# Expert down matrices stored slot by slot, with the two half tiles of neighbouring groups joined

## What is computed

```python
def expert(args):
    xe, wg, wu, wd = args              # 32 x 1024, 1024 x 2816, 1024 x 2816, 2816 x 1024
    a = jnp.einsum('bcd,df->bcf', xe, wg)
    u = jnp.einsum('bcd,df->bcf', xe, wu)
    return jnp.einsum('bcf,fd->bcd', jax.nn.silu(a) * u, wd)

out = lax.map(expert, (xin, w_gate, w_up, w_down))
```

## Time and profile before

| What | Value |
|---|---|
| Median of 3 runs | 2984.71 us |
| Lowest and highest run | 2976.73 and 2993.71 us |
| Span of the profiled execution | 2981.8 us |
| TensorE busy | 2348.0 us, 79% of the span |
| HBM read | 752.11 MB, 253 GB/s over the span |

### The profile page before, as it was taken

How to read it: one execution, slowest core, us unless ns; L and a number is a source line. 1 busy time by engine, 2 the same in 40 slices (tenths; PEclk the granted TensorE clock), 3 DMA queues, 4 the chain that set the end, 5 groups by cost and what they waited for, 6 DMA issues and landing times.

```text
span 2981.8 us, 36065 instructions
## 1 busy us (share of the span) xinstructions
PE 2348.0 (79%) x15206; PEld 1421.3 (48%) x15206; DVE 874.7 (29%) x1463; ACT 594.1 (20%) x964; POOL 63.1 (2%) x58
## 2 busy tenths in 40 slices
PE   6967767666666666777666789985899999868998
PEld 3844211111111111111111269972599799866997
DVE  6453000000000000000000044478455455554544
ACT  2410100000000000000000034410244454433443
POOL 0010000000000000000000000005100000000000
PEclk9977755555555555555555689996999999889999
DMA  5033899999999999999999955413245254321440
GB/s 219 15 145 137 293 387 402 392 373 371 370 391 394 390 372 377 374 396 401 368 380 374 390 224 190 147 37 155 85 170 183 105 223 180 142 120 64 173 180 32
DMA packets 110804, 754.27 MB, mean 253 GB/s; under 512 B 10791, under 2 KB 10952, under 8 KB 63432
## 3 DMA queue, kind: packets, MB, share of 16 engines
q1 hardware_dynamic: 107712, 748.20, 66.2%
q10 hardware_dynamic: 3016, 5.00, 0.5%
HBM read 752.11 MB, written 1.05 MB: 253 GB/s over the span
## 4 chain that ended last, share of the span: by engine, by line
PE 44%; DMA 27%; SPq 18%; DVE 8%; issue 1%; ACT 1%; POOL 0%; DVEq 0%; POOLq 0%; ACTq 0%
PE ps L1270 17%; SPq L963 11%; DMA work<-in_w_down 9%; DMA work<-in_w_gate 8%; PE ps L1281 8%; DMA work<-in_w_up 6%; SPq L966 5%; PE ps L773 3%; PE ps L423 2%; SPq L958 2%; PE ps L1836 2%; PE ps L988 2%; PE ps L1704 1%; PE ps L1013 1%; DMA ring<-in_w_up 1%
## 5 line engine op out<-in xcount | busy, mean ns | idle before, releaser
L988 PE MATMUL ps<-ring,arena 128*32 128x352 f32 x3072 | 452.9, 736 | 189.4 <-DMA ring<-in_w_gate 102.7
L1270 PEld LDWEIGHTS ps<-hsplit,w 128*128 128x128 f32 x4224 | 517.6, 192 | 6.2
L1270 PE MATMUL ps<-hsplit,w 128*128 128x256 f32 x4224 | 520.2, 283 | 0.0
L988 PEld LDWEIGHTS ps<-ring,arena 128*32 128x32 f32 x3072 | 110.1, 150 | 525.3 <-DMA ring<-in_w_gate 194.6
L1030 ACT ACTIVATE arena<-ps 128x352 f32<-128x352 f32 x32 | 13.1, 461 | 1312.1 <-PE ps L988 1312.1
L1040 DVE TENSOR_TENSOR arena<-arena,ps 128x352 f32<-128x352 f32 x32 | 15.2, 518 | 829.7 <-ACT arena L1030 829.7
L1281 PE MATMUL ps<-w,hidsplit 128*128 128x512 f32 x1056 | 255.3, 391 | 0.0
L1013 PE MATMUL ps<-work,arena 128*32 128x256 f32 (+1 forms) x1536 | 160.8, 567 | 104.0 <-DMA work<-in_w_down 103.9
L1013 PE MATMUL ps<-ring,arena 128*32 128x256 f32 (+1 forms) x1536 | 171.2, 597 | 76.0 <-DMA ring<-in_w_down 65.7
L1341 DVE TENSOR_TENSOR w<-ring,w 128x1024 fp32r<-128x1024 f32 x176 | 214.4, 1222 | 43.8 <-ACT w L1304 43.8
L1281 PEld LDWEIGHTS ps<-w,hidsplit 128*128 128x128 f32 x1056 | 192.9, 188 | 36.6
(11 more groups left out here) (379 smaller groups left out, 2112.5 us busy)
## 6 DMA issues: line engine op xcount, KB each, us to landing
ring<-in_w_gate SPq DMA_DIRECT2D x96, 1408.0 KB, 29.9
ring<-in_w_up SPq DMA_DIRECT2D x96, 1408.0 KB, 34.7
ring<-in_ffn_w SPq DMA_DIRECT2D x88, 1536.0 KB, 6.4
ring<-in_w_down SPq DMA_DIRECT2D x32, 1536.0 KB, 23.7
work<-in_w_down SPq DMA_DIRECT2D x32, 1536.0 KB, 24.5
work<-in_w_up SPq DMA_DIRECT2D x32, 1408.0 KB, 31.2
work<-in_w_gate SPq DMA_DIRECT2D x32, 1408.0 KB, 32.5
work<-in_w_down SPq DMA_DIRECT2D x32, 1024.0 KB, 23.0
```

The costliest lines, as they stand in the source:

```text
L988: last = pe.matmul(k.ps[32 * g:32 * g + CAP, 2 * w + half, 0:FH], xe[:, kk, :], slot(k, base + n)[:, g * FG + half * FH:g * FG + (half + 1 ...
L1270: last = pe.matmul(k.ps[:, 4 + c % 4, w * S:(w + 1) * S], k.w13[:, b, w, i, kk, :], k.hsplit[:, j, kk, :], start=(kk == 0 and n == 0), sto ...
```

## The change

The down matrices are laid out anew before the kernel starts (in `laid_out`, on the host's side, where other weights were laid out already). The half tile of group 0 and that of group 1 become one tile of 128 rows, and so do those of groups 2 and 3, so that an expert has 22 tiles where it had 24. They are dealt to eight slots with 3, 3, 3, 3, 3, 3, 2 and 2 tiles, and for each slot the bytes of a partition lie side by side: one run of 12,288 (or 8,192) bytes per partition, and one transfer per slot. TensorE gets one more transpose, VectorE one more copy of 64 x 96, both to have the second half of the joined tile's weights at partitions 64 to 127 of `hidT`, and the down product runs over 22 tiles. The bytes read are the same.

```diff
+DOWN_TILES = []
+for _g in (0, 2):
+    DOWN_TILES += [(_h, _m) for _h in (_g, _g + 1) for _m in range(FT)] + [(_g, FT)]
+DOWN_SLOTS = [(0, 3), (3, 3), (6, 3), (9, 3), (12, 3), (15, 3), (18, 2), (20, 2)]
...
-                    g, part = (n - 2 * DK) // 2, n % 2
-                    rows = FG * g + 3 * P * part
-                    whole = 3 - part
-                    sync.dma_start(s[:, 0:whole * D].rearrange("p (m d) -> p m d", m=whole),
-                                   w_down[0, bass.ds(e, 1), rows:rows + whole * P, :].rearrange("e (m p) d -> p (e m) d", p=P)).then_inc(ready, 16)
-                    if part:
-                        sync.dma_start(s[0:FR, 2 * D:3 * D],
-                                       w_down[0, bass.ds(e, 1), rows + 2 * P:rows + 2 * P + FR, :].rearrange("e p d -> p (e d)")).then_inc(ready, 16)
+                    first, tiles = DOWN_SLOTS[n - 2 * DK]
+                    sync.dma_start(s[:, 0:tiles * D], w_down[bass.ds(e, 1), first * P * D:(first + tiles) * P * D]
+                                   .rearrange("e (p f) -> p (e f)", p=P)).then_inc(ready, 16)
...
+            last = pe.transpose(k.ps[:, 5, 2 * P:3 * P], hidden[:, FG - P:FG], k.ident)
             last.then_inc(turned, 1)
...
-            for g in range(NG):
-                for m in range(FT + 1):
-                    n = 2 * DK + 2 * g + m // 3
-                    if m % 3 == 0:
-                        pe.wait_ge(k.ready(base + n), e * again[n] + mark[n])
-                    w = P if m < FT else FR
+            for n, (first, tiles) in enumerate(DOWN_SLOTS, 2 * DK):
+                pe.wait_ge(k.ready(base + n), e * again[n] + mark[n])
+                for i in range(first, first + tiles):
+                    g, m = DOWN_TILES[i]
                     for j in range(NG):
-                        last = pe.matmul(k.ps[32 * j:32 * j + CAP, 6, 0:256], hidT[0:w, m, 32 * g:32 * g + CAP],
...
+                        last = pe.matmul(k.ps[32 * j:32 * j + CAP, 6, 0:256], hidT[:, m, 32 * g:32 * g + CAP],
...
-                dve.tensor_copy(hidT[0:FR, 5, :], k.ps[0:FR, 5, P:2 * P]).then_inc(hidT_rest_put, 1)
+                dve.tensor_copy(hidT[0:FR, 5, :], k.ps[0:FR, 5, P:2 * P])
+                dve.tensor_copy(hidT[FR:P, 5, 0:P - CAP], k.ps[FR:P, 5, 2 * P + CAP:3 * P]).then_inc(hidT_rest_put, 1)
...
+    down = np.asarray(a["w_down"][0]).reshape(NE, NG, FG, D)
+    tiles = [down[:, g, m * P:(m + 1) * P] if m < FT else np.concatenate([down[:, g, FT * P:], down[:, g + 1, FT * P:]], 1)
+             for g, m in DOWN_TILES]
+    out["w_down"] = np.concatenate([np.stack(tiles[first:first + n], 2).reshape(NE, -1) for first, n in DOWN_SLOTS], 1)
```

More of the change, by code:

```diff
@@ L935, in experts @@
     per = 3 * DK
-    dmas = [1] * (2 * DK) + [1, 2] * NG
-    mark = [k.use.landing(base + n, dmas[n]) for n in range(per)]
-    again = [k.use.landing(base + per + n, dmas[n]) - mark[n] for n in range(per)]
+    mark = [k.use.landing(base + n) for n in range(per)]
+    again = [k.use.landing(base + per + n) - mark[n] for n in range(per)]
     for e in range(2, NE):
         for n in range(per):
-            k.use.landing(base + per * e + n, dmas[n])
+            k.use.landing(base + per * e + n)
     def load(sync):
@@ L1005, in expert @@
                 weighted_sums(k, pe, range(NG - 1))
-            for g in range(NG):
-                for m in range(FT + 1):
-                    n = 2 * DK + 2 * g + m // 3
-                    if m % 3 == 0:
-                        pe.wait_ge(k.ready(base + n), e * again[n] + mark[n])
-                    w = P if m < FT else FR
-                    for j in range(NG):
-                        last = pe.matmul(k.ps[32 * j:32 * j + CAP, 6, 0:256], hidT[0:w, m, 32 * g:32 * g + CAP],
[L1014 to L1017, removed]
+            for n, (first, tiles) in enumerate(DOWN_SLOTS, 2 * DK):
+                pe.wait_ge(k.ready(base + n), e * again[n] + mark[n])
+                for i in range(first, first + tiles):
+                    g, m = DOWN_TILES[i]
+                    for j in range(NG):
+                        last = pe.matmul(k.ps[32 * j:32 * j + CAP, 6, 0:256], hidT[:, m, 32 * g:32 * g + CAP],
+                                         slot(k, base + n)[:, (i - first) * D + j * 256:(i - first) * D + (j + 1) * 256],
+                                         start=(i == 0), stop=(i == len(DOWN_TILES) - 1))
+                if n < per - 1:
+                    last.then_inc(k.slot_freed, 1)
             last.then_inc(down_done, 1)
@@ L2253, in laid_out @@
     return out
-WHOLE = ["x", "filt_w1", "filt_w2", "filt_w3", "w_out", "w_router", "w_gate", "w_up", "w_down", "final_norm_g",
+WHOLE = ["x", "filt_w1", "filt_w2", "filt_w3", "w_out", "w_router", "w_gate", "w_up", "final_norm_g",
          "ple_w_gate_2", "ab_w_in_2",
```

## The result

The changed kernel takes 2826.08 us (median of 4 runs, 2824.92 to 2831.03) against 2986.39 us for the kernel before in the same comparison: a ratio of 0.9475, with a 95% interval from 0.9438 to 0.9511 (the two medians alone give 0.9463). The forecast was 2835 us, in a range from 2815 to 2876. The profiled execution of it spans 2823.2 us, 158.6 us less than that of before.

A forecast was written before the change was run, and what follows sets the result against it. DMA was taken to bound the kernel; faster down transfers would save 9.6 us per expert, 153 us over 16, less 3 us for edges. That 150 us off the 2984.7 us median gave 2835 us, range 2815 to 2876.

The forecast's parts named there:

- The bound: Expert stage: it lasts as long as its bytes take on DMA; down matrix at 314 GB/s, gate and up at 425.
- Part 1: Down matrix's four 64-row transfers per expert: they slow themselves and transfers around them, and joining them removes the slow windows.
- The own price: A 64-row transfer by itself: 256 KB at 190 GB/s takes 0.76 us too much, 3.0 us per expert.
- The dips' price: Four slow windows in the first expert's down transfers, 237 to 281 GB/s against 412: 6.3 us lost.
- engines out of step: Around 64-row transfers: DMA engines sharing the way to a partition fall out of step and disturb each other's next transfer.
- Part 2: Down transfers: runs of 12,288 bytes in place of 4096 raise the rate to 425 GB/s, worth 0.7 us per expert.
- The sum: Both parts over the down matrix: 36.7 - 27.1 = 9.6 us per expert, 153 us over 16 experts.
- the 3 us taken off for edges: Expert stage: an allowance for edges such as the first transfers after a pause, leaving a gain of 150 us.
- Part 4: Between up and down: one more transpose and copy, at most 8.5 us in all, taken as nothing because the ring covers it.
- Only the price of the transfers themselves: Rival for the down transfers: only 3.0 us plus 0.7 us per expert goes, 59 us, to 2926 us; chance 7%.
- The dips go, the rest stays: Rival for the down matrix: 2.6 us per expert stay, gain 112 us, to 2873 us; chance 8%.
- Slower by contiguous blocks: Rival for the down transfers: 1.5 MB blocks are served badly; at 250 GB/s, 150 us more, 3135 us; chance 2%.

The follow-up runs named there:

- e1: The changed kernel with down matrices laid tile by tile, so runs are 4096 bytes again, with joined tiles and one transfer per slot kept; 2843.98 us, ratio to before 0.9525.
- e3: The kernel before with its 64-row transfers written to partitions 32 to 95, not 0 to 63, half tiles' part of the result left out; 2844.56 us, ratio 0.9525.
- e5: The changed kernel with every down slot sent as two 64-row transfers, partitions 0 to 63 and 64 to 127; 3428.27 us in 2 runs.
- e8: The changed kernel with each expert's last down slot sent as two 64-partition halves, SP waiting before and after them in the first expert only; 2946.92 us, single run.
- e7: The changed kernel with the added transpose between up and down done 21 times in place of once; 2831.33 us.

## Why the prediction was right

**The bound.** DMA, and the rate within an expert: right. The gate and up slots stayed at 3.39 us, and the down matrix now takes 81.33 - 54.2 = 27.1 us, the very value of the sum.

**Part 1, the 64-row transfers.** Right in kind, and shown by e1 and e3 from two sides. They cost (2982.68 - 2843.98) / 16 = 8.7 us per expert. The own price was put at 3.0 us, from a row of 190 GB/s; at the 218 GB/s of e5 it would be 2.3 us. The dips' price was put at 6.3 us, and 2.6 us were in no window. Most of those 2.6 us belonged to the same transfers. The earlier trace rows end the down phase at 1083 us and go on at 1089 us, and the stretch between is slow too:

```profile
1083.00:1089.00 6.00, 3.86 (x36) 1.17 (x32) 0.00 (x0) 0.00 (x0) 0.00 (x0) 0.50 1.00 346
```

The two stretches, 36 us at 331 and 6 us at 346 GB/s, lose 8.0 and 1.1 us against 425 GB/s, so 9.1 of the 9.6 us can be seen. The windows of the earlier trace rows have gaps and were held against 412 GB/s, which made the dips look smaller. The reason for the dips (engines out of step) was put as a reading; e5 and e8 support it and don't prove it.

**Part 2, the long runs.** Mis-sized: 0.7 us per expert in the sum, 1.0 to 1.1 us by e1 against the changed kernel. The clean windows of 3 and 4 us from which the 411 to 417 were read are too short for a difference of 1%. That long runs would be worth nothing, which the prediction set against its rows, is ruled out by the 17.9 us. Since the sum took both parts together from the whole 36.7 us, the error shifts 0.4 us between them and nothing in the total.

**The sum.** The 153 us were right, and the 3 us taken off for edges were not. The expert stage starts at 311.31 us before and at 306.56 us after, and the first turn of the next stage, at L1218, at 1752.37 and 1594.31 us:

```profile
306.56 6.12 PE L988 MATMUL ps<-ring,arena 128*32 128x352 f32 x80 [2.02 <-POOL arena L976]
...
1594.31 5.81 PE L1218 MATMUL ps<-arena 128*128 128x128 f32 x32 [0.71 <-ACTq L143]
```

for the changed kernel, and for the kernel before

```profile
311.31 6.12 PE L988 MATMUL ps<-ring,arena 128*32 128x352 f32 x80 [2.02 <-POOL arena L976]
...
1752.37 6.19 PE L1218 MATMUL ps<-arena 128*128 128x128 f32 x32 [0.71 <-ACTq L137]
```

The stretch between shrank from 1441.06 to 1287.75 us, by 153.3 us. Of the other 5.3 us of the difference of the spans, 4.75 us lie ahead of the experts, in code that the change doesn't touch; the forecast had no term for that part. Traces of other kernels came down on either side (e1 starts the stage at 310.9 us and e3, with the layout of before, at 306.5), so that isn't an effect of the layout; what makes it stays open. These 4.8 us and the 3 us are most of the 9 us by which 2835 was too high. The lower end of the range doesn't follow from its own terms: a down stream at 430 GB/s gives 5 us and the scatter 8 us, so 2822 us and not 2815. The measured time lies within either.

**Part 4, the added transpose and copy.** Right, and by e7 with much room.

**The rivals.** *Only the price of the transfers themselves* would have left 2926 us; by e1 the loss is 8.7 us per expert and not 3.0. e3 shows that the place of the 64 rows is the cause, and the size is three to four times what their own bytes at half rate give. *The dips go, the rest stays* (2873 us) didn't happen either: the down matrix fell to 27.1 us, so nothing stayed. *Slower by contiguous blocks* didn't happen: 425 GB/s for the whole stage.

## What to carry to other kernels

In a stage bound by DMA, take the rate of each kind of transfer apart, in windows of a few microseconds, and don't trust the DMA share: it is 1.0 for a stream at half rate too. A load of 64 rows at partition 0 (or 64) among full ones costs more than its own excess, here between one and a half times (e5) and three to four times (the kernel before) as much; join two such loads to one of 128 rows, or, where what reads them allows it, write them to partitions 32 to 95. Longer runs per partition come second (1.1 us of 82.4 here).

## What was not expected of the hardware

- Where 64 rows are written changes the time of a kernel by 138 us (4.6%) with the same transfers otherwise: partitions 0 to 63 against 32 to 95.
- One 1 MB slot per expert sent as two halves of 64 partitions costs 4.4 us in the fastest run and 7.8 us in the median, with a scatter of 2896 to 2965 us between runs, while kernels without 64-row transfers at partition 0 or 64 scatter by 5 to 9 us. The kernel before scatters by 17 us and, in the other comparisons, by 29 and 53 us. A stream with such transfers among full ones is not only slower, it is less even. And their price can grow within one execution, from 27.6 to 52.0 us per expert in e5.
- TensorE's granted clock in the down phase was higher with the faster stream, 0.87 where the earlier trace rows show 0.50:

```profile
1062.00:1090.00 28.00, 16.11 (x199) 7.88 (x199) 2.56 (x8) 1.88 (x2) 0.00 (x0) 0.87 1.01 425
```

The later three-tile down slots in the timeline above take 1.50 us, where the first still takes 2.79. The mean over the long stretch rose from 0.55 to 0.60 only. Why the clock rose was not tested. It bought nothing, since TensorE waits for DMA at either clock.
